# A two-layer block on one core: the first attention scores laid between value products, and modulation sums asked for at later tiles

## The reference, cut to what matters

```python
mods = jnp.split(silu_c @ ada_w[l] + ada_b[l], 6, axis=-1)      # the modulation: shift, scale, gate, twice
h = rms_norm(x, norm_mix[l]) * (1.0 + sc1) + sh1                # 256 tokens of x; hc the same for 256 of the context
aq, ak, av, nq, nk, nv = split_cols(h @ w_in, widths)           # six products of 512 columns each
a  = diff_attention(...)      # 4 differential heads: softmax(q1 k1) - lam * softmax(q2 k2), times v
nb = neighbourhood_attention(...)   # 8 heads of 64 with a bias and a mask, times nv
y = jnp.concatenate([a, nb], axis=-1) @ w_out
...
h2 = rms_norm(x, norm_ffn[l]) * (1.0 + sc2) + sh2
x = x + g2 * expert_choice_ffn(h2, moe_router[l], moe_w1[l], moe_w3[l], moe_w2[l])
```

## Time and profile before

| | us |
|---|---|
| median of 3 runs (lowest, highest) | 1905.43 (1904.11, 1908.06) |
| the profiled execution, its own time | 1908.84 |
| its span in the trace | 1906.7 |
| PE busy | 1644.3 (86%) |
| DVE busy | 670.1 (35%) |
| ACT busy | 344.0 (18%) |
| mean granted clock of PE, share of full speed | 0.946 |

### The profile page before, as it was taken

How to read it: one execution, slowest core, us unless ns; L and a number is a source line. 1 busy time by engine, 2 the same in 40 slices (tenths; PEclk the granted TensorE clock), 3 DMA queues, 4 the chain that set the end, 5 groups by cost and what they waited for, 6 DMA issues and landing times.

```text
span 1906.7 us, 23333 instructions
## 1 busy us (share of the span) xinstructions
PE 1644.3 (86%) x9704; PEld 843.7 (44%) x9704; DVE 670.1 (35%) x1438; ACT 344.0 (18%) x847; POOL 49.9 (3%) x50
## 2 busy tenths in 40 slices
PE   6999998999989899899999989899998765566655
PEld 3744774447444674333333323265554432233322
DVE  1267839763341762322213113150453120111202
ACT  2222137311000661100000000020441000000000
POOL 1000200001000000000000000000000000000000
PEclk9999999999989999899999999999999887887877
DMA  9312239773352103599999999940338999999997
GB/s 373 133 45 89 91 139 419 321 297 131 120 215 108 45 1 133 204 428 427 428 428 427 427 428 427 426 197 28 133 133 372 427 427 427 427 428 426 427 427 303
DMA packets 39387, 538.15 MB, mean 282 GB/s; under 512 B 4362, under 2 KB 4618, under 8 KB 6644
## 3 DMA queue, kind: packets, MB, share of 16 engines
q1 hardware_dynamic: 38292, 531.32, 67.2%
q0 software_dynamic: 992, 5.36, 0.8%
HBM read 535.61 MB, written 1.05 MB: 281 GB/s over the span
## 4 chain that ended last, share of the span: by engine, by line
PE 55%; DMA 31%; DVE 9%; issue 2%; ACT 2%; DVEq 1%; SPq 0%; POOL 0%; POOLq 0%; ACTq 0%
PE bank L641 53%; DMA mem<-in_moe 28%; PE bank L651 2%; DMA mem<-in_ada_w 2%; DVE mem L1608 2%; DVE mem L1560 2%; DMA mem<-in_w_ada 1%; DVEq L1557 1%; DVE mem L1773 1%; DVE mem L1780 1%; ACT mem L2376 1%; DVE mem L2122 0%; DVE mem L1777 0%; POOL mem L2718 0%; DVE mem L2222 0%
## 5 line engine op out<-in xcount | busy, mean ns | idle before, releaser
L641 PE MATMUL bank<-mem 128*32 128x256 f32 (+14 forms) x8924 | 1534.4, 486 | 236.4 <-DMA mem<-in_moe 129.6
L641 PEld LDWEIGHTS bank<-mem 128*32 128x32 f32 (+4 forms) x8924 | 757.3, 148 | 943.0 <-issue 653.3
L2376 ACT ACTIVATE mem<-bank 128x512 f32<-128x512 f32 (+5 forms) x270 | 133.1, 504 | 1108.4 <-PE bank L641 725.0
L2122 DVE TENSOR_TENSOR mem<-mem,bank 128x512 f32<-128x512 f32 (+1 forms) x32 | 17.8, 556 | 489.9 <-PE bank L641 489.9
L2141 DVE TENSOR_TENSOR mem<-bank,mem 32x512 f32<-32x512 f32 (+1 forms) x120 | 66.7, 555 | 204.3 <-PE bank L641 203.1
L651 PE MATMUL bank<-mem 128*128 128x128 f32 x752 | 122.2, 289 | 17.7 <-DVE mem L2122 4.7
L651 PEld LDWEIGHTS bank<-mem 128*128 128x128 f32 x752 | 85.4, 145 | 101.8 <-issue 58.1
L1747 DVE SCALAR_TENSOR_TENSOR mem<-mem 128x256 f32<-128x256 f32 x160 | 86.9, 543 | 10.4 <-issue 0.9
L1608 DVE SCALAR_TENSOR_TENSOR mem<-mem 128x512 f32<-128x512 f32 x76 | 57.1, 752 | 30.8 <-DMA mem<-in_ada_w 14.7
L2718 POOL TENSOR_TENSOR mem<-mem 128x1 f32<-128x1 f32 (+5 forms) x20 | 16.2, 811 | 1329.4 <-DVE mem L1560 1329.4
L1560 DVE TENSOR_SCALAR mem<-bank,mem 128x128 f32<-128x128 f32 (+2 forms) x124 | 40.1, 393 | 26.3 <-PE bank L651 26.1
(11 more groups left out here) (204 smaller groups left out, 548.5 us busy)
## 6 DMA issues: line engine op xcount, KB each, us to landing
mem<-in_moe SPq DMA_DIRECT2D x190, 2048.0 KB, 34.9
mem<-in_ada_w SPq DMA_DIRECT2D x24, 2048.0 KB, 8.8
mem<-in_w_in SPq DMA_DIRECT2D x10, 2048.0 KB, 8.7
mem<-in_w_ada SPq DMA_DIRECT2D x6, 2048.0 KB, 12.6
mem<-in_even_w_in SPq DMA_DIRECT2D x6, 2048.0 KB, 8.4
mem<-in_w_out SPq DMA_DIRECT2D x4, 2048.0 KB, 11.8
mem<-in_odd_w_in SPq DMA_DIRECT2D x3, 2048.0 KB, 19.8
mem<-in_even_w_out SPq DMA_DIRECT2D x2, 2048.0 KB, 8.3
```

Of the source, the lines that this page charges most:

```text
L641: return nc.tensor.matmul(o, lhsT, rhs, start=start, stop=stop, skip_group_check=True)
L2376: took(name, S.activation(o, i, func))
```

## The change

On PE, the sums of steps 26 to 29 are asked for after `nq2`, `nk0`, `nk2` and `nv0` instead of after `nq1`, `nq2`, `nk0` and `nk1`. The scores of units 0 and 1 are asked for after `nv1`, those of units 2 and 3 after `nv2`. `router_bias(0)` moves from between `nv2` and `nv3` to behind the wait for `nv3`, and `router_bias_rows(0)` into the loop, at unit 2. On ACT, the exponentials of units 0 and 1 stand between the copies of `nv1` and `nv2`, those of units 2 and 3 between `nv2` and `nv3`. On DVE, the wait for `nv3` goes, and the two small router results are taken behind the first units. The functions `d_scores` to `unit_attend` (PE) stay as they are, ahead of the `nv` products in the text of the program.

```diff
@@ PE
-            SUM_AT = {"nq0": 25, "nq1": 26, "nq2": 27, "nk0": 28, "nk1": 29}
+            SUM_AT = {"nq0": 25, "nq2": 26, "nk0": 27, "nk2": 28}
...
             w = use("even5")
             for j in range(4):
                 t = B.open(f"nv{j}", "act")
                 B.close(t, token_major(t.ps[:, :], w, j, 0, 512))
-                if j == 2:
-                    router_bias(0)
+                if j == 0:
+                    ada_sum(29)
+                    wait_took(pe, "nk3")
+                    wait_took(pe, "kr3")
+                if j == 1:
+                    unit_scores(0)
+                    unit_scores(1)
+                if j == 2:
+                    unit_scores(2)
+                    unit_scores(3)
             done_with("even5")
-            router_bias_rows(0)
             wait_took(pe, "nv3")
-            wait_took(pe, "kr3")
+            router_bias(0)
...
-            for k in range(AHEAD):
-                unit_scores(k)
             for k, (kind, u) in enumerate(UNITS):
...
                 if k:
                     unit_attend(k - 1)
+                if k == 2:
+                    router_bias_rows(0)
@@ DVE
             router_scale(0)
-            router_bias(0)
-            router_bias_rows(0)
...
-            wait_took(dve, "nv3")
             d_max(0)
             dve.wait_ge(na_masked, 1)
             for k in range(1, AHEAD):
                 unit_max(k)
                 if k == 1:
                     combine(0)
+            router_bias(0)
             for k in range(len(UNITS)):
...
                     d_norm(k % per_tile // 2 - 2)
+                if k == 2:
+                    router_bias_rows(0)
@@ ACT
-            for j in range(4):
-                take(f"nv{j}", nv_tok[:, j, :], arrive(act, f"nv{j}")[:, :])
             wait_took(act, "kr3")
...
-            for k in range(AHEAD):
-                unit_exp(k)
+            for j in range(4):
+                take(f"nv{j}", nv_tok[:, j, :], arrive(act, f"nv{j}")[:, :])
+                if j == 1:
+                    unit_exp(0)
+                    unit_exp(1)
+                if j == 2:
+                    unit_exp(2)
+                    unit_exp(3)
```

More of the change, by code:

```diff
@@ L1084, in _ @@
                 done_with(f"even{i}")
-            w = use("even5")
-            for j in range(4):
-                t = B.open(f"nv{j}", "act")
-                B.close(t, token_major(t.ps[:, :], w, j, 0, 512))
-                if j == 2:
-                    router_bias(0)
-            done_with("even5")
-            router_bias_rows(0)
-            wait_took(pe, "nv3")
-            wait_took(pe, "kr3")
             def d_scores(u):
@@ L1145, in unit_attend @@
                     attend("n", u, 8, 64, nv_tok, u // 8, u % 8, att_T2[k % 2])
-            for k in range(AHEAD):
-                unit_scores(k)
+            w = use("even5")
+            for j in range(4):
+                t = B.open(f"nv{j}", "act")
+                B.close(t, token_major(t.ps[:, :], w, j, 0, 512))
+                if j == 0:
[8 more added lines that the diff above has]
+                    unit_scores(3)
+            done_with("even5")
+            wait_took(pe, "nv3")
+            router_bias(0)
             for k, (kind, u) in enumerate(UNITS):
```

## The result

The changed kernel takes 1888.8 us, the median of five runs (1888.22 to 1893.2), against 1905.43 before; one of the five runs of the kernel before beside it took 2808.17 us and is left out of the comparison. The ratio to the kernel before is 0.992 with a 95% interval of 0.9905 to 0.9934, so 12.6 to 18.1 us less. The medians are 16.6 us apart. The forecast was 1888.0 with a range of 1883 to 1898. The profiled execution took 1892.13 us with a span of 1889.9; the sum had said 1891.4.

A forecast was written before the change was run, and what follows sets the result against it. PE was taken to bound this stage wherever it does not wait. Removed waits and slow clock, 9.74 + 2.61 + 3.29 + 2.6, less 0.5 and 0.3, gave 17.4 us off the 1905.43 median: 1888.0 us, range 1883 to 1898.

The forecast's parts named there:

- the sum: All terms from nq2 into the loop: 9.74 + 2.61 + 3.29 + 2.6 - 0.5 - 0.3 = 17.4 us gained.
- The scores: Score pairs between nv1, nv2 and nv3: 0.5 us lost in all, bounds 0 and 1.
- The start of the loop: First transpose to end of twelve products: 6.71 us falls to 4.1 at full clock, 2.6 us gained.
- The small term that was wrong: router_bias_rows in the full loop instead of in the shadow of nv3's copy: 0.3 us lost.
- The router: DVE's router_scale, 8.7 us after PE's 29th sum, ends near 594.4; first scores are done near 594.
- The fourth rival: DVE's first minimum behind a late router load delays ACT, then PE: slower, 1909 or above; chance 0.02.
- That hole and the slow clock behind it: Between nq2 and nq3, PE's 5.82 us wait for a modulation pass plus 1.2 GHz after it: 9.74 us.
- the second hole: Between nk1 and nk2, PE's 2.54 us wait for a modulation pass: 10.23 against 7.62, 2.61 us gained.
- clock fall: Rival: clock still drops from nv1 to the loop; gain falls by 6 to 17, to 1894 to 1905; chance 0.08.
- The third: Rival: expert stages absorb the gain, nothing to some 5 us kept, 1900 to 1905; chance 0.07.
- The fifth: Rival: sums meet unfinished steps after a late slab; 3 us lost, 1891; chance 0.03.

The follow-up runs named there:

- the last experiment: Changed kernel with later wait for GpSimd's roots and PE's nv3 wait moved into the loop (1884.93 us), plus two unread products in a 1.73 us hole: 1884.33 us.

## Why the prediction was right

**The time.** The forecast's mechanism is borne out at each mark, with the profile's own shift of 1.35 us. nv0 was forecast at 585.22 and came at 586.57, which is 585.22 once the shift is taken off. The first transposes were forecast near 612.1 and came at 613.55, 612.2 without the shift. No sum is waited for; the clock is 1.00 throughout. The 17.4 us of the sum stand against 17.2 to the end of the heads in the traces and 16.6 between the medians.

**The scores.** Two pairs between nv1 and nv2 take 603.12 - 594.13 - 6.87 = 2.12 us and one pair between nv2 and nv3 8.12 - 6.87 = 1.25, so 3.37 us for three pairs of which each costs 0.92 in a row: 0.61 lost, where the sum had 0.5 and bounds of 0 and 1. The rule of the Trainium skill says that a switch of the tiling mode drains the array (TensorEngine Tiling (Array Packing), Key Properties). The trace agrees in sign, with 0.3 us for each way in and out; that the drain is what costs them is not shown.

**The start of the loop.** From the first transposes to the end of the twelve products takes 3.62 us, not 4.1: the gap for the copy is 0.34 us there, not 0.69, because ACT has nothing else queued. That term was 6.71 - 3.62 = 3.1 us and not 2.6. It is not the clock alone: in the kernel with both holes filled the clock there is full as well, but ACT's exponentials still stand ahead of the copy, and only 1.8 us are won.

**The small term that was wrong.** `router_bias_rows` in the loop was put at 0.3 us, and the stretch that holds it cost 1.07 us more than before. This, 0.8 us too small a cost, and the start of the loop, 0.5 us too small a gain, nearly cancel: that the sum of 17.4 lies only 0.2 us from the 17.2 is in part luck.

**The router.** From the memset to the end of router_scale were 592.84 - 587.11 = 5.7 us, against 585.95 - 577.56 = 8.4 before (the forecast's 8.7 counts from PE's sum, a little earlier). router_scale thus ended at 591.5 without the shift, not near 594.4, and DVE waited for the scores and not for the load. The fourth rival exists as a mechanism and was some 10.7 us away: 12.9 us later it costs 3.4 us between the medians.

**Where the working was weak.** "That hole and the slow clock behind it cost 17.52 - 7.78 = 9.74 us together", with 2.61 us added for the second hole, reads as if each could be had alone. The total is right (12.4 worked out, 12.2 measured) only because the change moves all of the sums. The filled hole shows it: the 3.9 us saved in front of sum 29 were lost there and more, since the chain of loads sets that point (576.8 before, 578.0 in that execution). The two terms are one: how much later than its own work PE is let past sum 29. The right question for each is what would be met next if only this one went.

**The other rivals.** No clock fall came between the value products (1.00 in every window from 540 to 690). The third (absorbed later) is ruled out: of the 17.2 us at the end of the heads the span keeps all. The fifth did not show, since no sum is waited for.

## What to carry to other kernels

An engine that waits on a paced chain (here PE, on loads that each start when the pass over the one before is done) should be asked for the chain's results after they are due, and the last of these waits is the one to move first: work won ahead of it only lengthens it. A hole on PE costs more than its length where the clock falls behind it, so count from a mark before the hole to a mark behind the slow stretch, not the idle time. Work that is ready early but written late (scores, their minima and exponentials) can be laid between long products, here at about 0.3 us for each insertion, if the queues of the engines that read it have slack; that slack can be measured by delaying the queue on purpose.

## What was not expected of the hardware

Filling a hole with unread work made the kernel slower by 3.9 us, while PE did everything up to the next wait faster; the full clock was won in a place where it was worth nothing.

The spread between executions of one kernel, some 4 us either way of the middle, can be seen in the clock far away from the change. Windows 50 to 100 and 350 to 400 of the changed kernel's profile, then of the last experiment's, in code that is the same in both:

```profile
50.00:100.00 50.00, 48.80 (x223) 37.88 (x222) 11.30 (x24) 10.21 (x18) 0.00 (x0) 0.97 0.34 126
350.00:400.00 50.00, 47.68 (x176) 21.35 (x168) 29.91 (x58) 8.65 (x23) 2.67 (x4) 0.93 0.78 313
```

```profile
50.00:100.00 50.00, 48.81 (x229) 37.69 (x228) 12.10 (x27) 10.95 (x19) 0.00 (x0) 1.00 0.34 126
350.00:400.00 50.00, 47.68 (x172) 22.34 (x173) 32.53 (x62) 7.80 (x21) 4.00 (x6) 1.00 0.79 323
```

PE's busy times are equal to 0.01 us, since a full engine is as busy at either clock, but the first ran part of both stretches at a lowered clock (0.97 and 0.93) and the other did not (1.00), and the first reached nq0 at 528.15, the other at 523.62, 4.5 us apart. The same holes meet a lowered clock in one execution and not in the next. This fits that single holes of 2 us, such as those at the end of the heads, could be seen in the traces and hardly in the medians.
